# A two-network kernel: grouped attention's query strips streamed one place earlier, and an older head's normalising sums inside the next key strip

## The reference, cut to what matters

```python
# first network, layer 1: each head
s = jnp.einsum("bhcqd,bhckd->bhcqk", q, k); p = softmax(s)
attn = p[:, :, 0] - lam * p[:, :, 1]
o = einsum(attn, v)
o = rms_norm(o, subln_g) * (1.0 - lam_init)      # over a head's 128 columns
y = (o * silu(g)) @ w_out
# second network, both layers: each head
q = apply_axial_rope_2(rms_norm_2(split_heads(q), q_norm_w), cos, sin)
attn = blocked_gqa(q, k_all, v_all)              # softmax(q k / sqrt(128)) v
y = concatenate([sgu * silu(za), merge_heads(attn) * silu(zb)]) @ w_out
```

## Time and profile before

| what | value |
|---|---|
| median of 3 runs | 2798.53 us (2798.18 to 2805.46) |
| profiled execution, its own time | 2805.79 us |
| its span in the trace | 2804.1 us |
| TensorE busy | 2639.0 us (94%) |
| VectorE busy | 2045.8 us (73%) |
| ScalarE busy | 1224.6 us (44%) |
| strips: matmuls on L249 to L251 | 3264 of each |

### The profile page before, as it was taken

The page is one execution under the profiler, slowest core; times in us unless marked ns, Lnnn a source line. Parts: engine busy times, 40 slices in busy tenths (PEclk is TensorE's granted clock), DMA queues, the critical chain, the costliest instruction groups (busy, mean ns, idle before and its releaser), DMA issues.

```text
span 2804.1 us, 39539 instructions
## 1 busy us (share of the span) xinstructions
PE 2639.0 (94%) x13490; PEld 2133.3 (76%) x13490; DVE 2045.8 (73%) x3196; ACT 1224.6 (44%) x1875; POOL 211.6 (8%) x402
## 2 busy tenths in 40 slices
PE   5799999999899999999989899999998997999989
PEld 1477777788677777777768788888886887998978
DVE  4399999999778788687877777764454666775655
ACT  3266556622443444444345433323444324544642
POOL 1110011011000000000000011100000100110000
PEclk8799999999999999999999899999999998999999
DMA  9765455476455565565655355532221643873325
GB/s 370 287 196 164 166 181 177 145 262 225 180 180 204 178 199 181 183 209 195 217 187 193 131 188 182 187 123 99 68 74 49 223 148 124 282 239 120 122 101 167
DMA packets 126557, 498.35 MB, mean 178 GB/s; under 512 B 14464, under 2 KB 16512, under 8 KB 116608
## 3 DMA queue, kind: packets, MB, share of 16 engines
q1 hardware_dynamic: 74176, 267.49, 27.7%
q0 software_dynamic: 52288, 229.66, 23.8%
HBM read 492.90 MB, written 4.19 MB: 177 GB/s over the span
## 4 chain that ended last, share of the span: by engine, by line
PE 75%; DVE 12%; issue 5%; DMA 4%; ACT 3%; DVEq 1%; POOL 0%; ACTq 0%; POOLq 0%; SPq 0%
PE psum L249 18%; PE psum L251 18%; PE psum L250 18%; PE psum L262 4%; DMA y<-in_mod_weights 2%; DVE w_lo L231 2%; PE psum L263 2%; DVE psum L409 2%; PE psum L299 2%; ACT w_hi L223 1%; PE psum L1631 1%; PE psum L1099 1%; PE psum L836 1%; DVE work L411 1%; PE psum L1645 1%
## 5 line engine op out<-in xcount | busy, mean ns | idle before, releaser
L249 PE MATMUL psum<-h_both,w_hi 128*128 128x512 f32 (+1 forms) x3264 | 1184.3, 363 | 5.6 <-DVE w_lo L231 5.6
L251 PE MATMUL psum<-h_both,w_lo 128*128 128x512 f32 (+1 forms) x3264 | 1156.1, 354 | 0.0
L250 PE MATMUL psum<-h_both,w_hi 128*128 128x512 f32 (+1 forms) x3264 | 1155.4, 354 | 0.0
L231 DVE TENSOR_TENSOR w_lo<-raw,w_hi 128x1024 fp32r<-128x1024 f32 x496 | 584.9, 1220 | 305.3 <-ACT w_hi L223 302.4
L249 PEld LDWEIGHTS psum<-h_both,w_hi 128*128 128x128 f32 x3264 | 619.6, 190 | 100.0 <-issue 13.2
L250 PEld LDWEIGHTS psum<-h_both,w_hi 128*128 128x128 f32 x3264 | 619.8, 190 | 92.4 <-issue 9.8
L251 PEld LDWEIGHTS psum<-h_both,w_lo 128*128 128x128 f32 x3264 | 619.1, 190 | 85.8
L223 ACT ACTIVATE w_hi<-raw 128x1024 fp32r<-128x1024 f32 x496 | 496.7, 1052 | 388.3 <-PE psum L251 301.4
L262 PE MATMUL psum<-h_both,w_hi 128*128 128x512 f32 x480 | 177.0, 409 | 10.0 <-DVE h_both L609 9.6
L263 PE MATMUL psum<-h_both,w_lo 128*128 128x256 f32 x480 | 137.0, 286 | 0.0
L409 DVE SCALAR_TENSOR_TENSOR psum<-y,modraw 128x1024 f32<-128x1024 f32 x98 | 120.3, 1228 | 21.1 <-DMA y<-in_mod_units 18.5
(11 more groups left out here) (289 smaller groups left out, 3127.3 us busy)
## 6 DMA issues: line engine op xcount, KB each, us to landing
raw<-in_weights SPq DMA_DIRECT2D x496, 512.0 KB, 4.4
y<-in_mod_units POOLq DMA_DIRECT2D x130, 512.0 KB, 4.2
modraw<-in_mod_weights POOLq DMA_DIRECT2D x48, 1024.0 KB, 5.5
work<-in_mod_units POOLq DMA_DIRECT2D x62, 512.0 KB, 4.6
y<-in_mod_weights POOLq DMA_DIRECT2D x16, 1024.0 KB, 9.1
xl<-in_mod_units POOLq DMA_DIRECT2D x32, 512.0 KB, 4.8
modraw<-in_mod_units POOLq DMA_DIRECT2D x32, 512.0 KB, 4.7
modraw<-in_cond_rows POOLq DMA_DIRECT2D x6, 1024.0 KB, 8.0
```

What stands on the lines that cost most here:

```text
L231: dve.tensor_tensor(w_lo[:, par, half, :], raw[:, 2 * par + half, :], w_hi[:, par, half, :].bitcast(F32), ALU.subtract).then_inc(S["split_ ...
L249: pe.matmul(dst, hi, h_hi[:, k, 0:n], start=(k == 0), stop=False)
L250: pe.matmul(dst, hi, h_lo[:, k, 0:n], start=False, stop=False)
L251: mm = pe.matmul(dst, lo, h_hi[:, k, 0:n], start=False, stop=(k == KT - 1))
```

## The change

In the first network's attention the older head's sum of squares (`sums`) moves from behind the scores to the middle of the key strip, and ScalarE's root of it (`root`) to the head of the round, followed by a one-element exponential (`warm`) ahead of the key strip's results. In rounds without a strip both stay where they were.

In the second network the order of the stream becomes q0, q1, z0, q2, z1, ..., q7, z6, z7 (z for gate). Round i now takes head i's query strip, and the gate strip, transposed weights and weighted sum of head i-1; one round follows the last head, not two. `sums(i)` stands between the query strip and the gate strip. The rotation and the scores of head i stand behind the gate strip. Rounds 0, 1 and 8 are written apart (`first`, `second`, `end`). What each instruction computes stays as it is.

```diff
+                def sums():
+                    pe.wait_ge(A["o_evac"], i - 1)
+                    pe.wait_ge(A["sdq"], min(i, HEADS1) if isinstance(i, int) else i)
+                    pe.matmul(psum[:, M_BANK, 0:T], ones, osq, start=True, stop=True).then_inc(A["sso"], 1)
+
+                def key_strip(half):
+                    if half:
+                        mod_chunk(pe, M_ATT + j, 2 * par)
+                    elif older:
+                        sums()
...
+                    strip(pe, att_strip(j, par, 0), psum[:, K_BANK, :], NT, key_strip)
                 if before:
...
-                if older:
-                    pe.wait_ge(A["o_evac"], i - 1)
-                    pe.matmul(psum[:, M_BANK, 0:T], ones, osq, start=True, stop=True).then_inc(A["sso"], 1)
+                if older and not here:
+                    sums()
...
+                def root():
+                    act.wait_ge(A["sso"], i - 1)
+                    act.activation(osq, psum[:, M_BANK, 0:T], ACT.Sqrt, scale=1.0 / P, bias=eps_col).then_inc(A["sdo"], 1)
+                if older and here:
+                    root()
+                    act.activation(warm, eps_col, ACT.Exp)
...
-                if older:
-                    act.wait_ge(A["sso"], i - 1)
-                    act.activation(osq, psum[:, M_BANK, 0:T], ACT.Sqrt, scale=1.0 / P, bias=eps_col).then_inc(A["sdo"], 1)
+                if older and not here:
+                    root()
...
+        def q_strip(lay, j, par):
+
+            first = isinstance(j, int) and 2 * j + par == 0
+            return Strip(S_NET2 + lay * L2_STRIPS + L2_ATT, 0 if first else 2 * par - 1, j, 4)
+
+        def z_strip(lay, j, par):
+
+            last = isinstance(j, int) and 2 * j + par == HEADS2
+            return Strip(S_NET2 + lay * L2_STRIPS + L2_ATT, 2 * par - 1 if last else 2 * par, j, 4)
 
...
+            def sums(h):
+                pe.wait_ge(B["q_evac"], base + h + 1)
+                ge(pe, B["sdq"], base + h)
+                pe.matmul(psum[:, 6, 0:n], ones, q2s[:, 0:n], start=True, stop=True).then_inc(B["ssq"], 1)
...
+                first, second, end = (isinstance(i, int) and i == m for m in (0, 1, HEADS2))
+                if here:
+                    ge(pe, B["q_evac"], base + i)
+                    strip(pe, q_strip(lay, j, par), psum[:, 0, 0:n], n, (lambda half: None if half else turned(0)) if second else None)
+                if second:
+                    scores(0, 0)
+                if before and not second and not end:
+                    turned_weights(i - 1)
+                if here:
+                    sums(i)
+                if before:
+                    ge(pe, B["sz"], base + i - 1)
+                    strip(pe, z_strip(lay, j, par), psum[:, 1, 0:n], n)
+                if second or end:
+                    turned_weights(i - 1)
+                if end:
                     pe.wait_ge(B["q_evac"], base + HEADS2)
                     pe.wait_ge(B["sz"], base + HEADS2)
                     out_first(pe, 2 + lay, 0, 4)
+                if here and not first:
+                    turned(i)
+                if before:
+                    weighted(i - 1, 1 - par)
+                if here and not first:
+                    scores(i, par)
...
+                first, second, end = (isinstance(i, int) and i == m for m in (0, 1, HEADS2))
+                if before and not second:
+                    exps(i - 1)
                 if here:
-                    st = gqa_strip(lay, j, par, 0)
+                    st = q_strip(lay, j, par)
                     act.wait_ge(S["strip_done"], st.s + 1)
                     next_strip(split_hi, act, st)
                     ge(act, B["qr"], base + i)
-                    if isinstance(i, int) and i == 0:
+                    if first:
                         act.wait_ge(B["v_t"], 2 * (lay + 1))
                     act.activation(q2[:, 0:n], psum[:, 0, 0:n], ACT.Copy)
...
+                if second:
+                    exps(0)
+                if before and not second and not end:
+                    weights(i - 1)
                 if here:
-                    st = gqa_strip(lay, j, par, 1)
+                    act.wait_ge(B["ssq"], base + i + 1)
+                    act.activation(q2s[:, 0:n], psum[:, 6, 0:n], ACT.Sqrt, scale=1.0 / P, bias=eps_col).then_inc(B["sdq"], 1)
+                if before:
+                    st = z_strip(lay, j, par)
                     act.wait_ge(S["strip_done"], st.s + 1)
-                    next_strip(split_hi, act, st)
-                    ge(act, B["y2"], base + i - 1)
-                    act.activation(sz3[par][:, 0:n], psum[:, 1, 0:n], ACT.Tanh, scale=0.5).then_inc(B["tz"], 1)
-            rounds(act, body, HEADS2, 2, 4)
+                    if end:
+                        split_hi(act, st.pair + 1, st.par, halves=(0,))
+                        to_high(act, 2 + lay, 0, 1)
+                        split_hi(act, st.pair + 1, st.par, halves=(1,))
+                        to_high(act, 2 + lay, 1, 3)
+                        weights(i - 1)
+                        to_high(act, 2 + lay, 3, 4)
+                        gate(i - 1, 1 - par)
+                        to_high(act, 2 + lay, 4, OUT_REST)
+                    else:
+                        next_strip(split_hi, act, st)
+                        gate(i - 1, 1 - par)
+                if second:
+                    weights(0)
+            rounds(act, body, HEADS2, 1, 4)
...
+                here, before = live(i, HEADS2), live(i - 1, HEADS2)
+                first, second, end = (isinstance(i, int) and i == m for m in (0, 1, HEADS2))
+                if second:
+                    rotated(0)
+                if before and not second:
+                    softmax(i - 1)
+                if here:
+                    next_strip(split_lo, dve, q_strip(lay, j, par))
+                if second:
+                    softmax(0)
+                if here:
+                    normed(i)
+                if here and not first:
+                    rotated(i)
                 if end:
-                    to_low(dve, 2 + lay, 10, 14)
...
+                    st = z_strip(lay, j, par)
+                    split_lo(dve, st.pair + 1, st.par, halves=(0,))
+                    to_low(dve, 2 + lay, 0, 1)
+                    split_lo(dve, st.pair + 1, st.par, halves=(1,))
+                    to_low(dve, 2 + lay, 1, 4)
+                    gate(i - 1, 1 - par)
+                    to_low(dve, 2 + lay, 4, 6)
+                    gated(i - 1, 1 - par)
+                    to_low(dve, 2 + lay, 6, OUT_REST)
+                elif before:
+                    next_strip(split_lo, dve, z_strip(lay, j, par))
+                    gate(i - 1, 1 - par)
+                    gated(i - 1, 1 - par)
+            rounds(dve, body, HEADS2, 1, 4)
...
-             + [c for h in heads for c in (q + h, zb + h)])
+             + [q + heads[0]] + [c for n in range(1, HEADS2) for c in (q + heads[n], zb + heads[n - 1])] + [zb + heads[-1]])
```

More of the change, by code:

```diff
@@ L1586, in gqa_pe, with turned, scores @@
             n = NT if wide_ else T
+            def turned(h):
+                pe.wait_ge(B["qn"], base + h + 1)
+                ge(pe, B["qt1"], base + h)
+                pe.matmul(psum[:, 5, 0:T], rot2, q2[:, 0:T], start=True, stop=True).then_inc(B["rotq"], 1)
+            def scores(h, kv):
+                if isinstance(h, int) and h == 0:
+                    pe.wait_ge(B["kr"], 2 * (lay + 1))
+                    pe.wait_ge(B["v_sb"], 2 * (lay + 1))
+                pe.wait_ge(B["qr"], base + h + 1)
+                ge(pe, B["attn_sb"], base + h)
+                keys = k2[kv]
+                for qt in range(2):
+                    mm = pe.matmul(psum[:, 2 + qt, :], q2r[:, qt * P:(qt + 1) * P], keys, start=True, stop=True)
+                if wide_:
+                    for qt in range(2):
+                        mm = pe.matmul(psum[:, 4, qt * T:(qt + 1) * T], q2r[:, T + qt * P:T + (qt + 1) * P], keys[:, T:NT],
+                                       start=True, stop=True)
+                mm.then_inc(B["scores"], 1)
@@ new lines, in weighted @@
+            def weighted(h, kv):
+                pe.wait_ge(B["attn_sb"], base + h + 1)
+                ge(pe, B["y2"], base + h)
+                for kt in range(4):
+                    mm = pe.matmul(psum[:, 7, 0:T], v2[kv][:, kt * P:(kt + 1) * P], at2[:, kt, :], start=(kt == 0), stop=(kt == 3))
+                if wide_:
+                    for kt in range(2):
+                        mm = pe.matmul(psum[:, 7, T:NT], v2[kv][:, T + kt * P:T + (kt + 1) * P], at2c[:, kt, :],
+                                       start=(kt == 0), stop=(kt == 1))
+                mm.then_inc(B["av"], 1)
@@ L1594, in body @@
                     out_first(pe, 2 + lay, 0, 4)
-                if end:
[L1596 to L1603, removed]
@@ L1617, in body @@
-                if here:
-                    ge(pe, B["sz"], base + i)
```

(16 more changed lines are left out.)

222 lines of the change are left out of this document (85 added, 137 removed).

## The result

The changed kernel takes 2814.36 us (median of 18 runs, 2802.06 to 2823.35) against 2804.25 us for the kernel before on the same chips: a ratio of 1.0034, 95% interval 1.0024 to 1.0043. It is slower by about 10 us. The profiled execution has a span of 2812.7 us, 8.6 us above the one before.

The account below looks back on a forecast made before the run. TensorE, busy 94% of the span, was taken as the bound. Attention -16.5, grouped attention +13.9 (layer 0) and +12.8 (layer 1), clock +10.5 sum to +20.7 us on 2798.5: 2819 us, range 2807 to 2830.

Parts of the forecast that it names:

- Mechanism and sign: Grouped attention: TensorE stops at the sum behind each query strip, 12 times about 2.2 us; whole kernel slower, chance 0.82.
- The short stop: Sum behind the query strip: `q_evac` comes early; below about 0.5 us a stop, over 0.3% faster (2790 us or less); chance 0.12.
- First attention: Key sum no longer waits for the root: -18.6 us, plus 14 x 0.15 for the moved sum, -16.5 us.
- Steady stops: Grouped attention, rounds 2 to 7: TensorE waits at the query sum, 13.2 us in layer 0, 12.6 us in layer 1.
- Rounds 0 and 1: Grouped attention's first rounds: waits at the query sums and weighted sum, 8.4 us in layer 0, 7.9 us in layer 1.
- Drains: Round 8: output tiles wait for the last head's gating, 6.0 us (was 13.7) in layer 0, 5.6 (was 10.3) in layer 1.
- The clock: Grouped attention: 12 stretches at half clock, 7 more than before, 1.5 us each: +10.5 us (bounds 0 and 19.5).
- The rival with the clock unchanged: Steady rounds of grouped attention: the clock stays as it is, +10.2 us in total, 2809 us; chance 0.16.

Follow-up runs that it names:

- the ladder: Two variants of the changed kernel on ScalarE: Copy and Square between the split's halves, 2790.01 us (0.9945); Square ahead of Copy, both behind the split, 2804.25 us (0.9993).

## Why the prediction was right, and where its terms were off

- **Mechanism and sign: right.** The stop at the sum, its cause (the two splits ahead of the Square) and its 12 places are as forecast, and moving either side of the race removes it. The short stop, the faster rival, did not happen; it is what the kernel with the Copy and Square ahead shows, and that one is faster.
- **First attention, -16.5 us: too small, -21.3 us measured.** That lies outside my bounds of -18.6 and -13.7. From the key strip's first matmul to the chunk of modulation, L299, it is 11.08 us before and 11.56 after, so the sum in mid-strip costs 0.48 us. From that chunk to the key sum it is 10.69 us before and 8.76 after, 1.93 us less: 0.43 us is the sum's old place (from the first score to the query strip's last matmul, 8.08 us before and 7.65 after), and 1.50 us is the wait (from that matmul to the key sum, 1.62 before and 0.12 after). With 0.08 us less at the restart behind the key sum that is 1.53 us a round, 14 times. So the move of the sum costs 0.05 us net, where I took 0.15. The term that I had too small is the wait: I took it from the profile, which counts it from a modelled end (1.33 us a round), and by distance of starts, restart included, it is 1.58 us.
- **Steady stops, 13.2 and 12.6 us: 11.2 us each by the profile's waits.** I counted the transposes ahead of the stop to the start of what follows them (0.88 + 0.35 us), but the profile's wait begins at their modelled end, 0.2 to 0.25 us later. By distance of starts a round of layer 0 without a fall of the clock grew from 29.6 to 31.7 us, 2.1 us or 12.7 in six, and one of layer 1 from 17.0 to 18.8 us, 1.9 us or 11.2 in six. So the first term was nearly right and the second 1.4 us too large.
- **Rounds 0 and 1, 8.4 and 7.9 us:** 7.5 us (3.14 + 0.57 + 3.81) and 7.0 us (2.72 + 1.00 + 0.49 + 2.78). **Drains, 6.0 and 5.6 us:** 5.8 and 5.0 us.
- **The clock, +10.5 us: right in sum, in part by luck.** Stretches at half clock in the two grouped attentions grow from 17.0 to 37.4 us, so 10.2 us are lost. Six of the 12 steady stops were followed by one, as assumed, but that half was a guess: it was 2 in layer 0 and 4 in layer 1, and none at all behind the ladder's stops of up to 1.65 us. Of the four long waits of rounds 0 and 1, for each of which I took one fall, two had one close by. The rival with the clock unchanged gives +10.2 us, very near the measured total, and is still wrong: the clock did fall, and a larger gain in attention and smaller losses in grouped attention made up for it.
- **The sum.** Grouped attention +29.9 us where +37.2 was forecast, attention -21.3 where -16.5 was: two errors of one sign, so the difference came out at half the forecast, +10 us instead of +20.7. That 2814 lies near 2819 is partly luck and owes something to the kernel before, which took 2804 us in these runs and 2798.5 in the three that the forecast started from.

The Trainium skill (TensorE: Matmul & The Clock Gate, A second HAM failure mode: psum-queue depth-cycling) tells of a kernel in which frequent short idle times between groups of matmuls made the clock fall and rise again and again. Here that held in part: repeated stops of 1.83 to 1.92 us were followed by a fall 13 times in 24, those of 1.71 to 1.80 us once in 14, 12 stops of 1.35 to 1.65 us and 12 of 0.9 us never.

What stays open is what else decides. The length of the stop does not do it alone: layer 1, with the same stops and shorter strips between them, fell more often (9 of 12 against 4 of 12), and the stop of 3.14 us at the query sum of round 0 in layer 0 was followed by no fall in the changed kernel, but by one where grouped attention alone was changed. Each rung is one profiled execution.

## What to carry to other kernels

When a strip's result is asked for sooner on one engine, look at what stands ahead of the answer in the other engine's list: here two passes of 1.1 us together stood behind 1.9 us of splitting, and moving them in front gave back 27 us. Price a reordering of a pipelined loop at its first and last rounds too; mending them gave 19 us, and in the profiled executions about half of the gain came with fewer stretches at half clock. A small net change can hide large parts: -21 and +30 us gave +10, and with both put right the same idea gives about -36 us.

## What the runs showed of the hardware

- The granted clock did not go by idle time in sum. TensorE idle for 9.6 of 110 us in stops of 1.6 us kept 1.00; idle for 10.5 of 182 us in stops of 1.85 us it read 0.98, and for 11.7 of 115 us in such stops 0.94. The shortest stretches at half clock (1.2 GHz) lasted 3.4 us, and a round with one was 1.5 to 1.7 us longer.
- An fp32 sum cost 0.43 us where it stood between other fp32 matmuls and an fp32r strip, and 0.48 us in the middle of an fp32r strip, though its own two matmuls advance TensorE by only 0.35 and 0.25 us there. In mid-strip the first matmul behind it takes 0.41 us to the next start, the later ones 0.23.
- A table load kept to its 1.28 us, with the next activation 1.29 us behind its start (947.96 to 949.25), in the new place too.
